# Biases, modulation loads and context products moved in a two-block kernel with 32 experts

## The reference

```
first block:   x += gate1 * (dilated + differential attention) @ w_out
               h2 = rms(x)*(1+scale2)+shift2 ; top 4 of 32 experts per token
               expert: gu = h @ w_gate_up[e] + b_gate_up[e]          (1024 -> 2048)
                       act = (clip(u)+1) * g*sigmoid(1.702 g)
                       y  = act @ w_down[e] + b_down[e]              (1024 -> 1024)
second block:  for l in 0, 1:
               mod  = silu(c) @ ada_w[l] + ada_b[l]      (6*1024 values; also for c_ctx)
               latents: p = h @ w_in[l]; attention over context and latents,
                        a gated unit (gelu), a 31-tap convolution with layer norm,
                        three gates, w_out, then a squared-relu MLP 1024 -> 4096 -> 1024
               the context (256 tokens) goes through the same in l = 0,
               and gives only keys and values in l = 1
```

## Time and profile before

| | |
|---|---|
| median of 3 runs | 3129.35 us (3128.22 to 3134.81) |
| the profiled execution's own time | 3139.97 us |
| its span | 3138.2 us |
| mean granted clock of PE | 0.979 |
| PE, DVE, ACT busy | 95%, 42%, 15% |
| HBM read | 741.68 MB |

### The profile page before, as it was taken

One profiled execution on the slowest core, in us unless ns is written; L12 is line 12 of the kernel. 1 busy time (PEld: TensorE's weight loads), 2 busy tenths in 40 slices (PEclk: granted clock), 3 DMA queues, 4 the chain that ended last, 5 costly groups with the idle time before them and its releaser, 6 DMA issues.

```text
span 3138.2 us, 30984 instructions
## 1 busy us (share of the span) xinstructions
PE 2965.7 (95%) x12068; PEld 1742.1 (56%) x12068; DVE 1325.8 (42%) x3177; ACT 476.8 (15%) x948; POOL 55.5 (2%) x85
## 2 busy tenths in 40 slices
PE   5997999999999999999889999999999999999998
PEld 3464345444555444544367768644444577587764
DVE  6755423566652121111326953273773258731201
ACT  1212001122212110010112031100000111311100
POOL 0000000000000000000000000000000000000000
PEclk9977999999999999999999999999999999999999
DMA  8554999999998988999943413343432244124342
GB/s 338 205 221 186 394 374 395 374 370 392 396 381 357 388 331 359 372 389 399 395 196 141 160 54 134 134 161 115 180 136 79 97 145 148 67 108 146 123 161 94
DMA packets 107297, 752.89 MB, mean 240 GB/s; under 512 B 12368, under 2 KB 12752, under 8 KB 18544
## 3 DMA queue, kind: packets, MB, share of 16 engines
q1 hardware_dynamic: 93888, 691.05, 55.8%
q0 software_dynamic: 6912, 46.14, 3.8%
q10 hardware_dynamic: 6352, 13.71, 1.2%
HBM read 741.68 MB, written 9.18 MB: 239 GB/s over the span
## 4 chain that ended last, share of the span: by engine, by line
PE 84%; DMA 9%; DVE 4%; ACT 1%; issue 1%; DVEq 0%; SPq 0%; ACTq 0%
PE ps L525 26%; PE ps L537 17%; PE ps L832 9%; DMA ring<-stream 9%; PE ps L747 8%; PE ps L913 7%; PE ps L743 3%; PE ps L1111 2%; PE ps L557 2%; PE ps L1099 1%; PE ps L839 1%; PE ps L586 1%; PE ps L1045 1%; PE ps L1025 1%; PE ps L847 1%
## 5 line engine op out<-in xcount | busy, mean ns | idle before, releaser
L525 PE MATMUL ps<-area,ring 128*128 128x256 f32 (+1 forms) x3328 | 822.1, 409 | 0.3
L525 PEld LDWEIGHTS ps<-area,ring 128*128 128x128 f32 x3328 | 634.8, 191 | 184.5 <-issue 108.1
L537 PE MATMUL ps<-ring,area 128*128 128x512 f32 x1216 | 528.4, 596 | 3.2 <-DVE area L2125 3.2
L832 PE MATMUL ps<-ring,area 128*64 128x512 f32 x2112 | 477.9, 598 | 36.4 <-DMA ring<-stream 35.4
L537 PEld LDWEIGHTS ps<-ring,area 128*128 128x128 f32 x1216 | 231.9, 191 | 290.2 <-issue 285.1
L832 PEld LDWEIGHTS ps<-ring,area 128*64 128x64 f32 x2112 | 146.6, 137 | 349.6 <-issue 265.4
L747 PE MATMUL ps<-area,ring 128*128 128x256 f32 x1152 | 254.7, 379 | 0.1
L913 PE MATMUL ps<-ring,area 128*64 128x512 f32 x1056 | 239.4, 606 | 6.9 <-ACT area L2357 5.2
L747 PEld LDWEIGHTS ps<-area,ring 128*128 128x128 f32 x1152 | 216.1, 190 | 28.2 <-issue 0.3
L1894 DVE SCALAR_TENSOR_TENSOR area<-area,cols 128x256 f32<-128x256 f32 x480 | 202.6, 485 | 1.1
L913 PEld LDWEIGHTS ps<-ring,area 128*64 128x64 f32 x1056 | 74.0, 139 | 152.3 <-issue 142.1
(11 more groups left out here) (344 smaller groups left out, 2153.4 us busy)
## 6 DMA issues: line engine op xcount, KB each, us to landing
ring<-stream SPq DMA_DIRECT2D x634, 1024.0 KB, 8.8
area<-shared_modulation POOLq DMA_DIRECT2D x40, 1024.0 KB, 6.9
area<-modulation SPq DMA_DIRECT2D x16, 1536.0 KB, 6.4
expert_rows<-area ACTq DMA_DIRECT2D x62, 128.0 KB, 7.4
x<-x_tiles ACTq DMA_DIRECT2D x1, 1024.0 KB, 12.5
area<-ctx_tiles ACTq DMA_DIRECT2D x1, 1024.0 KB, 4.8
out<-x SPq DMA_DIRECT2D x2, 512.0 KB, 2.6
cst<-constants ACTq DMA_DIRECT2D x1, 929.5 KB, 13.9
```

Source lines behind the costliest of these rows:

```text
L525: i = mm(ps[:, b, 0:n], w[:, k % 4, j * P:(j + 1) * P], rhs(k), start=(k == 0), stop=(k == 4 * kgs - 1))
L537: i = mm(ps[:, b, :], lhs(k, t), w[:, k % 4, :], start=(k == 0), stop=(k == 4 * kgs - 1))
L832: i = mm(ps[half(h), bank, :], xT[:, k % 4, half(k // 4)], w[:, 2 * (k % 2) + h, :], start=(k == 0), stop=False)
```

## The change

- **Biases.** `pickrow` holds the one-hot in all four groups of 32 partitions, `bgu` is 128x512 with a quarter of the columns in each group (four DMAs of 64 KB, nothing to clear). A new function `biases` stands ahead of both projections: four matmuls, each with 32 partitions in, 64 columns out, at four places of the array: gate halves and up halves. The projections then add to them. DVE writes the `pickrow` of the next expert once this block's biases are done.
- **PSUM.** The down projection of blocks 0 to 30 goes to bank 7 in place of the bank of the up projection.
- **Modulation.** Expert blocks 6 to 13 hold the chunks 8 to 15 of layer 0 (before, blocks 0 to 15 hold 8 to 23). Chunks 16 to 23 are loaded by POOL at the start of layer 0 of the second block; DVE does 12 of their 144 steps after each of the eight `cg` products and the other 48 in the first slots of `fill`. The coefficients of the MLP are made later, before the attention branch.
- **Taps.** At each head of attention `fill(3)`, in both layers.
- **Places.** The quota runs to the last block: the heavy steps lie in blocks 2 to 32, with two in block 31 and `("wo", 3)` in place A of block 32.

```diff
+LATE = 16
+SUMFROM = 6
-MOD_AT = [None] * FIRST + [at for e in range(NBLK) for at in mods_in(e)][:MODS - FIRST]
+MOD_AT = [None] * FIRST + [at for e in range(SUMFROM, NBLK) for at in mods_in(e)][:LATE - FIRST] + [None] * (MODS - LATE)
-            quota = -(-(2 * (e - START) + (w == "B")) * len(HEAVY) // (slots - 3))
+            quota = -(-(2 * (e - START) + (w == "B")) * len(HEAVY) // slots)
-        bgu = v(B1 + 10240, 2 * D)
+        bgu = v(B1 + 10240, 512)
+        modsm = [modsl[0], v(20960, KD, MODC * P)]
...
-                               start=(k == 0), stop=False)
+                               start=False, stop=(k == KD - 1))
-                if name == "gate":
-                    pe.wait_ge(*at((tag, "row")))
-                for h in range(2):
-                    i = mm(ps[half(h), bank, :], pickrow, bgu[:, 256 * first + 512 * h:256 * first + 512 * h + 512],
-                           start=False, stop=True)
+            def biases(tag, before):
+                pe.wait_ge(*before("row"))
+                for n in range(4):
+                    r = slice(NE * n, NE * n + NE)
+                    i = mm(ps[half(n % 2), (GATE, UP)[n // 2], :], pickrow[r, :], bgu[r, :], start=True, stop=False)
+                i.then_inc(*mark("biases_added", (tag, "bias")))
...
+                apart = e is not None and e < STORED
+                if e is None or e > STORED:
+                    pe.wait_ge(*before("y"))
+                biases(tag, before)
                 project(tag, e, "gate", GATE, 0)
...
-                        i = mm(ps[half(h), DOWN, :], actT[:, k % 4, half(k // 4)], w[:, 2 * (k % 2) + h, :],
+                        i = mm(ps[half(h), APART if apart else DOWN, :], actT[:, k % 4, half(k // 4)], w[:, 2 * (k % 2) + h, :],
...
+                if upcoming:
+                    dve.wait_ge(*at((tag, "bias")))
+                    pick_row(tag, e + 1)
...
-                    coefficients(0)
+                    coefficients(0, (0,))
+                def middle_sums():
+                    for m in range(LATE, MODS):
+                        dve.wait_ge(later_landed[m % 2], 16 * (1 + (m - LATE) // 2))
+                        yield from modulation_steps(m, modsm[m % 2], part2l, part2lt)
+                middle = middle_sums() if l == 0 else iter(())
                 for k in range(KD):
                     (glp product of k)
+                    for _ in range(12):
+                        next(middle, 0)
...
                 def fill(n):
-                        if next(taps, 0) == 0:
+                        if next(middle, 0) == 0 and next(taps, 0) == 0:
...
-                    fill(1)
+                    fill(3)
+                if l == 0:
+                    take_sums(MODS // MODG - 1)
+                    coefficients(0, (1,))
                 for f in range(4):
                     take_one("attn", f)
```

More of the change, by code:

```diff
@@ L866, in expert @@
                     pe.wait_ge(*before("sums_read"))
+                apart = e is not None and e < STORED
+                if e is None or e > STORED:
+                    pe.wait_ge(*before("y"))
+                biases(tag, before)
                 project(tag, e, "gate", GATE, 0)
-                if e != 0:
+                if e is not None and 0 < e <= STORED:
                     pe.wait_ge(*before("y"))
+                if scattered and upcoming:
+                    pe.wait_ge(*at((tag, "row")))
                 if scattered:
@@ L1499, in modulation_chunk, with modulation_steps @@
             def modulation_chunk(m, w, part2, part2t):
+                for _ in modulation_steps(m, w, part2, part2t):
+                    pass
+            def modulation_steps(m, w, part2, part2t):
                 for k in range(KD):
@@ L1721, in take_rows, with pick_row @@
                 STT(yacc[:, t, :], came[n % 4], kept[:, t, j:j + 1], yacc[:, t, :], ALU.mult, ALU.add).then_inc(*mark("rows_taken", ("taken", n)))
+            def pick_row(tag, e):
+                dve.wait_ge(*last("row_picked"))
+                V.tensor_copy(pickrow, onehot[:, bass.ds(e, 1)].to_broadcast([P, CAP])).then_inc(*mark("row_picked", (tag, "row")))
             def expert(tag, e, before, scattered, weighed, upcoming, main, work):
@@ L1792, in _ @@
             iotae_b = con("iotae", NE).unsqueeze(1).unsqueeze(1).to_broadcast([P, TT, TOPK, NE])
+            V.tensor_copy(pickrow, onehot[:, 0:1].to_broadcast([P, CAP])).then_inc(*mark("row_picked", (first, "row")))
             places()
@@ L1819, in _ @@
                     choose(("first", tag), 0)
+                    dve.wait_ge(*at((("moe", NBLK - 1), "bias")) if p == 1 else last("row_picked"))
+                    V.tensor_copy(pickrow, onehot[:, 0:1].to_broadcast([P, CAP])).then_inc(*mark("row_picked", (("first", tag), "row")))
                     dve.wait_ge(*at((("first", tag), "rows")))
@@ L1830, in _, with coefficients @@
             V.tensor_copy(stat("done"), flag[:, 0:1]).then_inc(*mark("x_updated", *[("x2", t) for t in range(TT)]))
[L1833 removed]
+            def coefficients(l, parts):
                 dve.wait_ge(*last("modulation_read"))
[L1836 to L1839, removed]
[L1840 to L1847 removed]
+                for second in parts:
+                    f0, f1, scale, gain, gate_ = ((0, 24, 8, "mix", 16), (24, 48, 32, "ffn", 40))[second]
+                    for s in range(2):
+                        TT_(modb[:, s, f0:f1], mod2[:, l, s, f0:f1], col(("ada_b", l), f0, 24), ALU.add).then_inc(*mark("vector_steps"))
+                        dve.wait_ge(*last("vector_steps"))
+                    for s in range(2):
+                        STT(aff[:, 2 * second + s], modb[:, s, scale:scale + 8], 1.0, col((gain + "_pre", l), 0, 8), ALU.add, ALU.mult).then_inc(*mark("vector_steps"))
+                        dve.wait_ge(*last("vector_steps"))
+                        TT_(aff[:, 4 + 2 * second + s], modb[:, s, gate_:gate_ + 8], col((gain + "_post", l), 0, 8), ALU.mult).then_inc(*mark("vector_steps"))
+                        dve.wait_ge(*last("vector_steps"))
             def modulated(name, spans, sh):
@@ L1926, in _ @@
                 i.then_inc(*mark("normed", (L, "gvn")))
+                for _ in middle:
+                    pass
                 if l == 0:
@@ L2117, in _ @@
                     later_sums(2 * MODS // MODG - 1)
-                    coefficients(1)
+                    coefficients(1, (0, 1))
                 for g in range(2):
@@ L2364, in expert @@
                     act.wait_ge(rows_stored, 32 * min(store[0], STORED))
-                A(ysb, ps[:, 1, :], ACT.Identity).then_inc(*mark("outputs_ready", (tag, "y")))
+                A(ysb, ps[:, 7 if store and store[0] < STORED else 1, :], ACT.Identity).then_inc(*mark("outputs_ready", (tag, "y")))
                 if store and store[0] < STORED:
```

51 lines of the change are left out of this document (23 added, 28 removed).

## The result

The changed kernel takes 3111.06 us (median of 4 runs, 3110.84 to 3112.07) where the kernel before took 3131.89 on the same chip (4 runs): a ratio of 0.9932, 95% interval 0.9917 to 0.9947, or 20.8 us less. On a second chip the pair was 3112.69 to 3136.0, a ratio of 0.9930 (0.9917 to 0.9943); one of the 13 runs of the kernel before took 4515.79 us there, at a granted clock of 0.652, and is not in the ratio. The prediction was 3108.7. The profiled execution after lies 1.0 us above its median, that of before 8.1 above the median of all its four runs: the two spans differ by 28.0 us, and some 7 of these are not the change's. So lengths of stages are taken from the traces here, and what a part is worth from times where both exist.

A forecast was written before the change was run, and what follows sets the result against it. PE was taken to bound the kernel (busy 2965.7 of 3138.2 us), with DMA limiting some blocks. Terms -20 - 12 - 5 + 4 + 2 + 15 - 4.7 = -20.7 took the median 3129.35 to 3108.7 us; range 3088 to 3131.

The forecast's parts named there:

- Expert stage, -37 predicted: Expert blocks: the biases, modulation and places terms together, -20, -12 and -5 us.
- Biases, -20: Four bias matmuls side by side ahead of the projections: 0.66 us saved per block, times 33 is 22, taken as 20.
- My lower bound, 8: Smallest gain of the biases term, if DMA holds a third of the blocks and the overlap is worse.
- The share of 0.92 to 0.95: DMA share at which the ring is loaded in most expert blocks, cited for the rival that DMA holds them.
- Modulation, -12: Loads leave blocks 0 to 5, 14 and 15, cutting PE's chunk waits: 12 us gained (5 to 17).
- Places, -5: Heavy steps moved to blocks 31 and 32: 19 us gained, 14 paid there; bounds -12 to +3.
- `cg` and gelu, +4: Layer 0, second block: modulation steps after `cg` products start DVE's gelu late; about 4 us lost (0 to 9).
- Attention, +2: Two more taps per head on DVE in attention: 2 us lost for both layers (0 to 5).
- Layer 0's wait for taps, +15: 32 taps move behind layer 0's fourth output, 49 in a row: +13.7 us on PE, 1 more for the clock; 12 to 18.
- Layer 1, -4.7: 16 taps move ahead in layer 1, so PE's wait for taps goes: 4.7 us gained.
- DMA keeps what PE gives: Expert-stage rival: shorter blocks only turn PE's work into chunk waits; +10 us, or 3139; decides under 22 us returned; chance 0.13.
- Biases in pairs or serial: Bias rivals: only column pairs overlap, +6 us, 3135, chance 0.05; or none overlap, +62, 3191, chance 0.01.

The follow-up runs named there:

- `u_mod`: The change with its modulation part undone (chunks 8 to 23 of layer 0 in blocks 0 to 15 again); ratio 0.9907 to the kernel before.
- `u_bias`: The change with the biases alone put back (two matmuls of 128 partitions close each projection); median 3123.02 us, ratio 0.9958 to the kernel before.
- `u_fill`: The change with `fill(1)` in place of `fill(3)` at each head of attention, both layers; ratio 0.9953 to the kernel before.
- `bias_one_group`: The change with its four bias matmuls all on the same 32 partitions; ratio 0.9970 to the kernel before.
- `fix_taps`: The change plus one line, `fill(43)` in layer 0 ahead of the attention branch's first output; 3087.96 us, ratio 0.9859 to the kernel before.
- `fix_place`: The change plus `fill(43)` in layer 0, with `slots - 1` for `slots` (quota ends one place earlier); 3088.46 us, ratio 0.9845 to the kernel before.

## Why the prediction held, and which terms did not

The forecast was 3108.7 us, the result 3111.06, inside its range and on its side. That it came within 2.4 us is in part luck, because errors cancel: the expert stage gave back less than I took (30 to 35 us of 37), and the second block took less (9.6 us with one trace of the change and 12.6 with the other, where +4 + 2 + 15 - 4.7 = 16.3 were forecast).

- **Expert stage, -37 predicted.** The traces say -38, but the profiled run of before is some 8 us above the median. By the times, the whole less the second block, it is -20.8 - 9.6 = -30 on the first chip and some -35 on the second. The undone parts have biases 8, modulation 10, places 3, in all 21; some 10 us I can't give to a part, and since the trace of `u_mod` puts 20.8 us on the modulation, they may well be there.
- **Biases, -20: the mis-sized term.** The working was right to 0.04 us: 0.66 a block predicted, 0.70 measured, and all of it from different partitions. The multiplication was wrong: I took the saving for nearly all of the 33 blocks. The times of four kernels put the term at 4 to 12 us and their traces at 11 to 19, none at 20. It counts in full in blocks 14 to 18, by half or more in 19 to 31 and not at all in 0 to 5, where the clock in blocks 0 and 1 is slower in the change's traces. My lower bound, 8, was nearer than my 20. The share of 0.92 to 0.95 beside most stretches could have warned me, since the average over a stretch mixes blocks at the stream's limit with blocks that have room; but fewer waits for chunks account for 5 to 8 us in two traces and for nothing in `u_bias`, so the reason for the rest stays open.
- **Modulation, -12:** 10 in time, 12 in blocks 1 to 5 of the trace, 20.8 in the trace of the whole stage. Right, or too small. Waits up to 523 us fell from 13.3 to 6.0 and not below 4.
- **Places, -5:** 3 in time. Right in size; the wait for ACT behind the product was 4.93 us where 5 was said. But the step in block 32 is a loss of 1.9 by itself, and those in block 31 earn it.
- **`cg` and gelu, +4:** nothing. `u_fill` has all the modulation steps there and takes the 299.7 us of before up to `mu`; PE's waits on DVE in these parts are under 1 us in all (0.2 in the page's row of L528). I gave PE's four banks too little slack. **Attention, +2:** 1 to 2, seen in layer 0.
- **Layer 0's wait for taps, +15:** +12.8 and +14.0 in two traces (37.7 us to 50.5 and 51.7), with a wait of 17.4 us where 18 to 20 were to be seen. Right, by the step predicted: 49 taps in 19.95 us where 21.0 was worked out.
- **Layer 1, -4.7:** -6.6, in every trace with `fill(3)`. The wait was 4.7, and with it went the slower clock behind it, which I had counted in layer 0 alone.
- **The rivals.** "DMA keeps what PE gives" had the size of the biases' term, 8, and not the rest: waits for chunks fell in the gate and up projections from 35.4 to 14.9 us over the whole, and the stage returned more than the 22 us at which it was to decide. Biases in pairs or serial are ruled out by `bias_one_group` (1.87 us) beside the 1.02. Of the cited rules, the Trainium skill (TensorE: Matmul & The Clock Gate, Part 3) with its 3.07 times for four row tiles would give, as an estimate, 3.44 / 3.07 = 1.12 us for the four; the rows show 1.02.

## What to carry to other kernels

A saving per block is multiplied by the blocks that the shortened engine bounds, and these are counted block by block (gather to gather), not from the mean share of a stretch. In this kernel small matmuls with few partitions paid when they lay on different partitions (1.02 us for four), and on the same ones they did not (1.87); they were issued together each time, and apart was not tried. Work that is dealt out in slots behind a program-order engine needs a look at that engine's longest idle time: one line that filled it was worth 24.7 us, as much as the whole change.

## What the runs showed of the hardware

These two pauses of PE cost more than their length. Stretches in the kernel before (pause of 4.7 us, then the time behind it):

```profile
1888.00:1893.00 5.00, 0.36 (x2) 0.00 (x0) 5.00 (x14) 0.00 (x0) 0.00 (x0) 1.00 0.62 236
1893.00:1897.00 4.00, 3.91 (x11) 3.21 (x12) 2.19 (x7) 0.88 (x3) 0.00 (x0) 0.58 0.01 4
1897.00:1902.00 5.00, 5.00 (x25) 4.41 (x24) 1.43 (x5) 2.27 (x7) 0.00 (x0) 1.00 0.00 0
```

and in the change (17.4 us):

```profile
1852.00:1869.00 17.00, 0.00 (x0) 0.00 (x0) 17.00 (x44) 0.00 (x0) 0.00 (x0) 0.62 0.15 59
1869.00:1874.00 5.00, 4.72 (x13) 3.90 (x14) 3.20 (x10) 1.69 (x6) 0.00 (x0) 0.60 0.02 3
1874.00:1880.00 6.00, 6.00 (x29) 5.28 (x29) 0.62 (x2) 1.84 (x6) 0.00 (x0) 1.00 0.00 0
```

Behind either pause the granted clock is at 0.6 for 4 to 5 us, mostly its lower level of 1.2 GHz, and then full again: two matmuls take 2.07 us where they take 1.13 without the pause. So the price is about 2 us whether PE stood for 4.7 us (6.6 us less in layer 1 for a wait of 4.7) or for 17.4 (19 to 20 less for `fix_taps`). I had expected a short pause to be free of it. What makes the clock fall is not worked out here: in block 32 of `fix_place` PE pauses 2.26 and then 0.69 us ahead of the down projection, which takes 9.87 us, and in the kernel before it pauses as long and the projection takes 7.09.

Four f32 matmuls of 32 partitions and 64 columns on four different places take 1.02 us where a pair on two column halves takes 0.86: they run side by side almost whole, and the change of shape is 0.10.
